# Expert stage of a transformer block: its beginning in another order

## The reference, cut to what matters

```python
q = (x @ w_query).reshape(T, PEER_HEADS, PEER_KEY_DIM)          # 1024 -> 8 x 256
s1 = einsum('thd,nd->thn', q[..., :half], sub_keys1)            # 128 scores each
s2 = einsum('thd,nd->thn', q[..., half:], sub_keys2)
v1, i1 = top_k(s1, 16);  v2, i2 = top_k(s2, 16)
cand = v1[..., :, None] + v2[..., None, :]                      # 256 sums
top_s, top_p = top_k(cand, 16)
e_idx = take(i1, top_p // 16) * 128 + take(i2, top_p % 16)
gate = softmax(top_s)
...
u = take(expert_u, ic);  act = gelu(einsum('cd,ced->ce', xc, u))
vv = take(expert_v, ic)
return einsum('ce,ced->cd', gc * act, vv)
```

## Time and profile before

| | us |
|---|---|
| median of 3 runs | 2150.65 (2150.57 to 2153.54) |
| profiled execution | 2146.91 |
| its span (first to last instruction) | 2145.1 |
| first gather issued | 408.3 |
| last dot begins | 1064.7 |
| next stage's first work | 1072.0 |

### The profile page before, as it was taken

The page is one execution under the profiler, slowest core; times in us unless marked ns, Lnnn a source line. Parts: engine busy times, 40 slices in busy tenths (PEclk is TensorE's granted clock), DMA queues, the critical chain, the costliest instruction groups (busy, mean ns, idle before and its releaser), DMA issues. The chain is left out here.

```text
span 2145.1 us, 33417 instructions
## 1 busy us (share of the span) xinstructions
PE 1856.9 (87%) x12148; PEld 1391.5 (65%) x12148; DVE 1485.9 (69%) x2618; ACT 1026.6 (48%) x2065; POOL 435.1 (20%) x457
## 2 busy tenths in 40 slices
PE   4974997898887777787799989889999999779998
PEld 4842887744442222222289988579998988668997
DVE  7676555787776676665466676766677787776666
ACT  2444213554544444444365554467665545435554
POOL 0010220144544344344200000002131330210000
PEclk8987998899999999999999999699999999889999
DMA  9860001599999999999855555035555655224552
GB/s 335 297 228 25 3 3 61 214 416 421 421 421 421 421 421 421 421 420 421 349 170 187 187 192 173 1 128 186 183 179 177 195 177 177 94 96 156 191 186 98
DMA packets 104386, 497.31 MB, mean 232 GB/s; under 512 B 11857, under 2 KB 17233, under 8 KB 71377
## 3 DMA queue, kind: packets, MB, share of 16 engines
q1 hardware_dynamic: 66064, 225.41, 31.4%
q0 software_dynamic: 36864, 268.45, 30.1%
q10 hardware_dynamic: 1344, 1.96, 0.3%
HBM read 494.73 MB, written 1.05 MB: 231 GB/s over the span
## 5 line engine op out<-in xcount | busy, mean ns | idle before, releaser
L247 PE MATMUL ps<-srcs,wh 128*128 128x512 f32 x2064 | 741.7, 401 | 22.7 <-DVE srcs L261 20.4
L1926 PE MATMUL ps<-row,diag 128*128 128x512 f32 x1024 | 498.1, 622 | 114.4 <-ACT diag L2030 114.4
L249 PE MATMUL ps<-srcs,wl 128*128 128x256 f32 x2064 | 582.5, 282 | 0.0
L229 DVE TENSOR_TENSOR wl<-ring,wh 128x1024 fp32r<-128x1024 f32 x362 | 452.3, 1252 | 120.0 <-ACT wh L223 118.8
L247 PEld LDWEIGHTS ps<-srcs,wh 128*128 128x128 f32 x2064 | 392.6, 190 | 114.6 <-issue 27.1
L1926 PEld LDWEIGHTS ps<-row,diag 128*128 128x128 f32 x1024 | 182.9, 193 | 417.4 <-ACT diag L2030 259.0
L2131 DVE CUSTOM_DVE_ANT_0 row<-row,h_tok 128x1024 f32<-128x1024 f32 x256 | 313.5, 1225 | 191.5 <-DMA row<-in_peer_uv,experts 179.2
L223 ACT ACTIVATE wh<-ring 128x1024 fp32r<-128x1024 f32 x362 | 379.2, 1052 | 65.4 <-PE ps L249 43.3
L249 PEld LDWEIGHTS ps<-srcs,wl 128*128 128x128 f32 x2064 | 395.3, 192 | 2.5 <-issue 2.4
L1839 POOL DMA_INDIRECT row<-in_peer_uv,experts x256 | 278.9, 1090 | 385.6 <-PE ps L1926 348.9
L2023 ACT ACTIVATE acts<-dots 128x1 f32<-128x1 f32 x256 | 51.8, 202 | 327.9 <-DVE dots L2131 327.1
(11 more groups left out here) (520 smaller groups left out, 2172.0 us busy)
## 6 DMA issues: line engine op xcount, KB each, us to landing
ring<-in_stream SPq DMA_DIRECT2D x378, 512.0 KB, 3.5
alpha<-in_ada_late SPq DMA_DIRECT2D x12, 512.0 KB, 5.1
beta<-in_ada_late SPq DMA_DIRECT2D x10, 512.0 KB, 5.1
kappa<-in_ada_late SPq DMA_DIRECT2D x10, 512.0 KB, 6.1
row<-in_peer_uv,experts POOLq DMA_INDIRECT x256
bias<-in_attn_bias SPq DMA_DIRECT2D x8, 256.0 KB, 5.7
w<-in_cmp_w SPq DMA_DIRECT2D x1, 2048.0 KB, 7.4
xT<-in_xT SPq DMA_DIRECT2D x1, 1024.0 KB, 15.1
```

What stands on the lines that cost most here:

```text
L229: nc.vector.tensor_tensor(wl[:, n % PAIRS, :], ring[:, tile % RING, :], wh[:, n % PAIRS, :].bitcast(F32), ALU.subtract).then_inc(tiles_fre ...
L247: nc.tensor.matmul(out, wh[:, n, cols], source.rearrange("p a t -> p (a t)"), start=start, stop=stop, skip_group_check=True)
L249: return nc.tensor.matmul(out[:, 0:S], wl[:, n, cols], source[:, 0, :], start=False, stop=stop, skip_group_check=True)
L1926: last = nc.tensor.matmul(y_part(t, half), diag[:, s % DIAGS, :], row[:, s % ROWS, D + half * 512:D + (half + 1) * 512], start=(slot == 0) ...
```

## The change: what it does

Nothing is added or removed; instructions of the stage's beginning stand in another order.

- VectorE: hT is made right behind choice 0; then `out(2)`, `weight(3)`, the gates, `out(3)`. Dots 0 and 1 stand in front of choice 1. Choice 1's first call does dot 2, and the second low parts (`split_again`) stand behind it. `weight` and `out` of queries 4 to 7 go from slot numbers 1, 2, 9, 13 to 6, 8, 12, 14; the gates of head 1 from slot 10 to 11. Nine dots instead of seven stand before choice 2.
- TensorE: `turn_h` stands between queries 2 and 3; queries 4 to 7 stand behind slots 2, 4, 8, 10, and `score(2)` behind slot 6.
- ScalarE: the exponential of head 0's gates and `h_tok` come before `copy_low(3)` and the scores of head 1. The second high parts stand behind slot 1, the work for queries 4 to 7 behind slots 4, 6, 10, 12, the scores of head 2 behind slot 8, the exponential of head 1 in front of slot 9.

```diff
@@ -1902,11 +1902,9 @@
                 pe.wait_ge(keys_in, 16)
                 score(0)
                 query(2)
+                turn_h()
                 query(3)
                 score(1)
-                turn_h()
-                query(4)
-                query(5)
 
                 def turn(t):
                     pe.wait_ge(query_out, T_QUERY)
@@ -1930,11 +1928,15 @@
                             last.then_inc(half_summed, 1)
                     last.then_inc(v_used, 1)
                     ahead = ahead_of(s // TOPK)
-                    if s == 1:
+                    if s == 2:
+                        query(4)
+                    if s == 4:
+                        query(5)
+                    if s == 6:
                         score(2)
-                    if s == 4:
+                    if s == 8:
                         query(6)
-                    if s == 8:
+                    if s == 10:
                         query(7)
                     if s == 13:
                         score(3)
@@ -1998,26 +2000,21 @@
                     nc.scalar.activation(hT[:, k, :], rstd[:, :], ACT.Copy, scale=mod[:, 24 + k:25 + k]
                                          ).then_inc(shifted, 1)
                 copy_low(2)
-                weight_and_copy(3)
+                high(act, first + AHEAD + 3)
                 gate_exp(0)
-                copy_scores(1)
-                act.wait_ge(tiles_used, split_no(first + UNSHIFTED - 1) + 1)
-                for k in range(KT):
-                    act.wait_ge(normed, k + 1)
-                    nc.scalar.activation(srch[:, k, :], hT[:, k, :], ACT.Copy).then_inc(second_high, 1)
                 for t in range(TT):
                     act.wait_ge(h_turned, t + 1)
                     nc.scalar.activation(h_tok[:, t, :], ps[:, 2 * t:2 * t + 2, :].rearrange("p b n -> p (b n)"),
                                          ACT.Copy, scale=rstd_tok[:, t:t + 1]).then_inc(h_copied, 1)
-                weight_and_copy(4)
-                weight_and_copy(5)
+                copy_low(3)
+                copy_scores(1)
                 for s in range(TT * SLOTS):
                     t, slot, head = s // SLOTS, s % SLOTS, s // TOPK
                     if slot % TOPK == 0:
                         if LOOKAHEAD <= head + 1 < HEADS:
                             gate_exp(head + 1)
                         act.wait_ge(gates_done, head + 1)
-                    if s == 8:
+                    if s == 9:
                         gate_exp(1)
                     act.wait_ge(dotted, s + 1)
                     nc.scalar.activation(acts[:, s:s + 1], dots[:, s:s + 1], ACT.Gelu).then_inc(gelued, 1)
@@ -2030,11 +2027,18 @@
                     nc.scalar.activation(diag[:, s % DIAGS, :], mat("ident"), ACT.Copy, scale=weights[:, s:s + 1]
                                          ).then_inc(diag_ready, 1)
                     ahead = ahead_of(s // TOPK)
-                    if s == 3:
+                    if s == 1:
+                        for k in range(KT):
+                            nc.scalar.activation(srch[:, k, :], hT[:, k, :], ACT.Copy).then_inc(second_high, 1)
+                    if s == 4:
+                        weight_and_copy(4)
+                    if s == 6:
+                        weight_and_copy(5)
+                    if s == 8:
                         copy_scores(2)
-                    if s == 7:
+                    if s == 10:
                         weight_and_copy(6)
-                    if s == 11:
+                    if s == 12:
                         weight_and_copy(7)
                     if s == 15:
                         copy_scores(3)
@@ -2184,18 +2188,20 @@
                 weight(2)
                 dve.wait_ge(counted, 1)
                 choose(0, lambda: None)
-                out(2)
-                weight(3)
-                out(3)
                 for k in range(KT):
                     dve.wait_ge(shifted, k + 1)
                     nc.vector.scalar_tensor_tensor(hT[:, k, :], xT[:, k, :], gs[:, 1, k:k + 1], hT[:, k, :],
                                                    ALU.mult, ALU.add).then_inc(normed, 1)
+                out(2)
+                weight(3)
                 finish_gates(0)
-                for k in range(KT):
-                    dve.wait_ge(second_high, k + 1)
-                    nc.vector.tensor_tensor(srcl[:, k, :], hT[:, k, :], srch[:, k, :].bitcast(F32), ALU.subtract
-                                            ).then_inc(second_low, 1)
+                out(3)
+
+                def split_again():
+                    for k in range(KT):
+                        dve.wait_ge(second_high, k + 1)
+                        nc.vector.tensor_tensor(srcl[:, k, :], hT[:, k, :], srch[:, k, :].bitcast(F32), ALU.subtract
+                                                ).then_inc(second_low, 1)
                 for head in range(HEADS):
                     slot, calls = counter(), counter()
 
@@ -2204,14 +2210,16 @@
                         slot.one()
                         if slot.now == 6 and LOOKAHEAD <= head + 1 < HEADS:
                             finish_gates(head + 1)
-                        if slot.now == 10 and head == 0:
+                        if slot.now == 11 and head == 0:
                             finish_gates(1)
                         if slot.now == 10 and head == NH:
                             add_out(0)
                         ahead = ahead_of(head)
-                        if head == 0 and slot.now in (1, 2, 9, 13):
-                            weight(4 + (1, 2, 9, 13).index(slot.now))
-                            out(4 + (1, 2, 9, 13).index(slot.now))
+                        if head == 0 and slot.now == 3:
+                            split_again()
+                        if head == 0 and slot.now in (6, 8, 12, 14):
+                            weight(4 + (6, 8, 12, 14).index(slot.now))
+                            out(4 + (6, 8, 12, 14).index(slot.now))
                         if ahead < NH and slot.now in (8, 13):
                             weight(2 * ahead + slot.now // 13)
                             out(2 * ahead + slot.now // 13)
@@ -2220,8 +2228,10 @@
                         if calls() % (4 if head == 0 else 2) == 1 and slot.now < TOPK:
                             next_dot()
                     if head == 0:
+                        next_dot()
+                        next_dot()
                         choose(1, meanwhile)
-                        while slot.now < 7:
+                        while slot.now < 9:
                             next_dot()
                     if head + LOOKAHEAD < HEADS:
                         choose(head + LOOKAHEAD, meanwhile)
```

## The result

| | before | changed |
|---|---|---|
| median of 20 runs, us | 2148.46 (2145.66 to 2153.54) | 2152.47 (2146.25 to 2156.31) |
| ratio, 95% interval | | 1.0017 (1.0010 to 1.0023) |
| profiled execution and its span, us | 2146.91, 2145.1 | 2147.56, 2145.6 |
| first gather issued | 408.27 | 407.69 |
| last dot begins | 1064.72 | 1065.62 |

The changed kernel is a little slower: its median is 4.0 us higher, and by the ratio it is 3.7 us, just inside the 0.2% that the prediction took as no change. The profiled execution is one of the fastest four of its twenty, so its span says little. The way from the first gather to the last dot leaves out what the stages ahead add (the first gather lies between 407.7 and 415.0 us in the fourteen profiles of this study).

A forecast was written before the change was run, and what follows sets the result against it. The prediction took DMA, at 2.48 us per gathered row, to bound the expert stage. It took the small losses at gathers 8, 11 to 14 and 24 as +0.5, giving 2151.2 us on the runs' median, range 2147.5 to 2156.0.

The forecast's parts named there:

- The first gather: Start of the expert stage: the gather follows choice 0, everything before it stays as it was, so 0 gained or lost.
- The engine steps: Chain behind choice 0: waits of 7.4 at `out(3)` and 2.4 at the split, gather 8 at 430.0, gather 24 at 477.1.
- GB/s never under 380 for 5 us: Sign of being right: the DMA transfer rate would not fall below 380 GB/s for 5 us.
- Rival 2: TensorE's clock stays half through query 3, so gather 8's packets come late: 3.3 us lost, 2154.2 us; chance 0.10.
- The ledger's ceiling: DMA account of the expert stage: no order gains more than 3.9 us unless the first gather starts earlier.
- Each version has about one microsecond of slack, so the earlier gather brings nothing; tiles moved later take its place: At gather 8: packets at 431.8 against 432.4 for the queued work; before, 433.3 against 434.9.
- the 3.5 us of losses: Time before slot 19's dot that the DMA account left unexplained: ramp, instruction transfers or idle; a third counted before gather 8.
- gather 8, up to 0.6 lost or as much gained: Term for the first reuse of slot 0: gather issued at 430.0 instead of 431.5, up to 0.6 us either way.
- gathers 11 to 14, 0 to 0.4: Term for the gathers that reuse slots 3 to 6: 0 to 0.4 us lost.
- Gather 24, 0 to 1.5: Term for the reuse of slot 16: issue at 477.1 instead of 469.74, cushion down to 0.4, 0 to 1.5 us lost.
- Rival 1: Ring of rows runs dry at slots 16 to 24, gather 24 after 477.5: 4 us more, 2155.2 us; chance 0.14.
- Rival 3: The 3.5 us before slot 19 were idle time, of which 2.5 could be gained: 2148.2 us; chance 0.12.

The follow-up runs named there:

- Kernel 6: The changed kernel with its front part undone (hT, gates and turns placed as in the kernel before); way 657.05 us, ratio 1.0003.
- Kernels 7 and 9: 7: changed kernel with query 6's tile split before the slots, ratio 1.0008; 9: changed kernel with TensorE's queries 4 and 5 behind slots 4 and 6, 1.0046.
- kernel 2: The kernel before with nine row buffers instead of eight; way 656.82 us, ratio 0.9996.
- Kernel 12: The kernel before run again without any edit; way 656.85 us, ratio 0.9997.

## Why the prediction was right, and where it wasn't

**The time.** Part of its success is luck. Forecast were 0.5 us more on a median of 2150.65 from three runs; twenty runs of the same kernel have 2148.46. So 2151.2 came near the measured 2152.47 though the change was 4.0 us by the medians and not 0.5. By the ratio it stays under the 0.2% by 0.6 us. That the effect is small and that DMA sets the end was right; the size was three to four times too small for the stage and left out what lies beyond it.

**The bound.** Right. From slot 27 on the dots wait for DMA as before, the slices are at 419 to 422 GB/s, and from slot 76 to the last dot every profile takes 449.2 to 449.6 us.

**The first gather.** It moved by 0.6 us, with everything ahead of it; in the others it lies up to 7 us later. The profiles don't tie this to the change.

**The engine steps.** Counted from the first gather's issue: gather 8 at 21.7 by the prediction, 21.45 measured; dot 15 at 59.9, measured 58.4; gather 24 at 68.8, measured 67.7. The wait at `out(3)` was 6.15 instead of 7.4, that at the split 2.10 instead of 2.4. The main error is on the safe side: the clock came back at 414, not at 416.8, so query 3 was done near 418.7, not 420.5. Of the prediction's signs of being right, the two waits, gather 8, gather 24 and the last dot came; "GB/s never under 380 for 5 us" did not (357 and 378), and slot 31's dot came 95.0 us after the first gather where it was 93.5.

**Rival 2, the half clock.** Wrong here for query 3. The query steps behind the turns are 0.35 apart from 414.39 on, which is the full level, 2.4 GHz. The Trainium skill, TensorE: Matmul & The Clock Gate, "Part 1: The HAM clock gate", has it that the half rate is left after sustained work. The trace agrees: the granted clock reads 0.50 until 414, and between 410.61 and 414 TensorE did nothing but the turns. The half clock shows elsewhere, at the first products. It reads 0.50 in every microsecond from 424 to 431 (TensorE had nothing but eight score products between 418.7 and 425.09), and twelve product records take 8.37 us; at the full clock twelve took 5.32 in the kernel before. The kernel before had full clock until 427.6 and from 430.7 on:

```profile
425.00:430.00 5.00, 2.25 (x4) 1.14 (x4) 4.93 (x18) 4.25 (x11) 0.00 (x0) 0.73 1.01 417
433.68 5.32 PE L1926 MATMUL ps<-row,diag 128*128 128x512 f32 x12
```

Slot 0 pays little for it (425.09 to the issue at 429.14 is 4.05 us, before 3.68), but slot 1 and the beginning of slot 2 run at the half clock as well, and gather 9 comes 2.87 us behind gather 8 where it was 1.72. The prediction hadn't looked there. (Its price for rival 2, 2154.2, doesn't follow from its own terms either: 3.3 us more are 2154.0 on the runs' median and 2154.5 on the forecast.) Kernel 6 has the same half clock (twelve in 8.14 us) and no hole, so the clock alone isn't the cause either; no run isolates its part.

**The ledger's ceiling.** It held: nothing gained more than 3.9 us, and nothing gained at all. That is weak evidence for its terms.

**The step that failed** is "Each version has about one microsecond of slack, so the earlier gather brings nothing; tiles moved later take its place". It stood on a third of the 3.5 us of losses as work ahead of gather 8. Without it, and with the execution's earlier start, eight rows and one tile are through at 430.6, and gather 8's packets come at 429.14 + 1.8 = 430.9. That is no slack at all, and gathers 9 and 11 were issued 2.9 and 4.1 us behind the ones before them, while a row takes 2.48. The term "gather 8, up to 0.6 lost or as much gained" together with "gathers 11 to 14, 0 to 0.4" measured 0.9 against the kernel before in the mean of the profiles (1.3 against a full rate in the first). "Gather 24, 0 to 1.5" measured 0.2, and gathers near 19, which the sum left out, 0.4. "First gather 0" left out the 0.5 lost 5 to 10 us behind it. The sum, forecast 0.5, is 1.6 for the stage by the mean of the ways, 1.9 at slot 33, and 2.0 by the MB moved in 80 us (32.44 against 31.60).

**Rival 1, the ring dry at slots 16 to 24.** Its mechanism is real, its place was wrong for the greater part: 0.9 us are lost behind gathers 8 to 11, where the prediction saw slack, and 0.6 at slots 16 to 24. Kernels 7 and 9 show larger holes there. **Rival 3**, that 2.5 us could be gained, is refuted by kernel 2, where the ring is fuller and nothing is gained. Kernel 12 has no dip at 35 to 40 us behind the first gather (424 GB/s, in the profile that the prediction read 386, and 378 in the earlier trace rows); it is 0.85 us ahead at slot 33 and 0.4 behind at the last dot. So such a dip comes and goes in the same kernel. What else the 3.5 us are, work, ramp or another loss, no run shows.

The whole program's difference, 3.7 us in the first series and 1.1 and 3.4 in the others (1.0005 and 1.0016 of 2149), is 0.7 to 2.3 times the stage's 1.6. The part beyond the stage isn't explained.

## What to carry to other kernels

Where a stage is bound by a queue with a fixed number of buffers, compare each new issue with the time at which the queue will be empty, not with its old issue time; and count side transfers that fill the queue while the buffers are all taken, since they are free there and may cost up to their length later. Don't enter a loss of unknown kind in such an account as work. When a step shared by three engines is moved, move all three shares, and try the halves of a reordering alone: here one cost 6.4 us, the other 0.4, both together 1.6.

## What the runs showed of the hardware that I had not expected

- The same kernel's profiled executions reach the first gather between 407.7 and 411.2 us (changed kernel, three profiles). This scatter is larger than the stage's loss.
- The granted clock rose at 414.0 in the changed kernel, when TensorE had been at the turns from 410.61 on, and at 420.5 in the kernel before, where the turns began at 414.79.
- The same kernel can meet the same work at either clock. The kernel before did its first eight products in 5.12 us in one profile (clock 0.73 in that stretch) and in 3.70 in kernel 12 (clock 1.00), and there gather 8 was issued 1.0 us earlier after the first.
- At much the same slots one row takes about 3.45 instead of 2.48 us (102, 131, 155, 184 and 212 in nearly all profiles). An earlier one comes at slot 74 or 75 in most, and in some one more at slot 51. What it is was not tested.
